# A fused Fourier-mixing and feed-forward block on one core: the second shift vector is summed in halves of 1024 columns, six of its sixteen units later, and two sums of mixing weights sooner

## The reference, cut to what matters

```python
mod_x = (silu(c) @ w_ada + b_ada)              # 2048 -> 6*2048
sh1, sc1, ga1, sh2, sc2, ga2 = split(mod_x, 6)
h = rmsnorm(x, g_mix) * (1 + sc1) + sh1
f = fftn(h.reshape(1, 512, 4, 512), axes=(1, 3), norm='ortho').real
x = x + ga1 * (f.reshape(1, 512, 2048) @ w_mix)
h2 = rmsnorm(x, g_ffn) * (1 + sc2) + sh2
x = x + ga2 * (square(relu(h2 @ w_in)) @ w_out)  # 2048 -> 8192 -> 2048
return rmsnorm(x, g_final)
```

## Time and profile before

| | us |
|---|---|
| median of 3 runs (lowest, highest) | 1658.37 (1655.5, 1659.79) |
| the profiled execution's own time | 1658.63 |
| its span | 1656.4 |
| PE busy, share of the span | 1602.9 (97%) |
| DVE busy | 1263.7 (76%) |
| ACT busy | 545.5 (33%) |
| clock of PE, mean of the span | 0.99 of full |

### The profile page before, as it was taken

The page is one execution under the profiler, slowest core; times in us unless marked ns, Lnnn a source line. Parts: engine busy times, 40 slices in busy tenths (PEclk is TensorE's granted clock), DMA queues, the critical chain, the costliest instruction groups (busy, mean ns, idle before and its releaser), DMA issues.

```text
span 1656.4 us, 18306 instructions
## 1 busy us (share of the span) xinstructions
PE 1602.9 (97%) x6989; PEld 1232.9 (74%) x6989; DVE 1263.7 (76%) x1148; ACT 545.5 (33%) x658; POOL 16.8 (1%) x30
## 2 busy tenths in 40 slices
PE   6899989899999999999999999999999999999996
PEld 5653323688888888888888888888888888888875
DVE  6649998448888888886868686867677777777878
ACT  5320002443333333333333333333333333333332
POOL 0000000100000000000000000000000000000000
PEclk9999999999999999999999999999999999999998
DMA  9999998713535454432323232322323333333342
GB/s 356 369 394 374 413 350 347 274 52 113 193 121 184 130 175 137 143 127 78 125 82 120 93 110 101 101 101 101 101 101 101 101 101 101 101 103 100 116 189 102
DMA packets 94921, 272.63 MB, mean 165 GB/s; under 512 B 4332, under 2 KB 5660, under 8 KB 80924
## 3 DMA queue, kind: packets, MB, share of 16 engines
q1 hardware_dynamic: 91616, 249.91, 42.1%
q0 software_dynamic: 3120, 22.07, 3.7%
q10 hardware_dynamic: 144, 0.07, 0.0%
HBM read 263.64 MB, written 8.39 MB: 164 GB/s over the span
## 4 chain that ended last, share of the span: by engine, by line
PE 86%; DVE 9%; DMA 2%; issue 2%; ACT 0%; SPq 0%; DVEq 0%; POOL 0%; ACTq 0%
PE banks L1234 16%; PE banks L1236 16%; PE banks L1235 16%; PE banks L1534 11%; PE banks L1538 11%; PE banks L1536 11%; DVE acc_a L802 4%; DVE acc_b L802 2%; DMA raw<-in_w_ada 1%; DVE mixw L900 1%; PE banks L1467 1%; PE banks L1252 1%; DMA xres<-in_x 0%; DVE gated L955 0%; DVE xres L959 0%
## 5 line engine op out<-in xcount | busy, mean ns | idle before, releaser
L1092 DVE TENSOR_TENSOR stp<-raw,stp 128x1024 fp32r<-128x1024 f32 x330 | 402.5, 1223 | 156.8 <-ACT stp L673 154.3
L673 ACT ACTIVATE stp<-raw 128x1024 fp32r<-128x1024 f32 x330 | 343.7, 1056 | 523.4 <-PE banks L1236 233.9
L1234 PE MATMUL banks<-acts,stp 128*128 128x512 f32 x1024 | 399.6, 390 | 0.0
L1235 PE MATMUL banks<-acts,stp 128*128 128x512 f32 x1024 | 398.4, 389 | 0.0
L1236 PE MATMUL banks<-acts,stp 128*128 128x512 f32 x1024 | 398.4, 389 | 0.0
L1538 PE MATMUL banks<-stp,hid 128*128 128x512 f32 x840 | 326.8, 389 | 0.0
L1536 PE MATMUL banks<-stp,hid 128*128 128x512 f32 x840 | 326.8, 389 | 0.0
L1534 PE MATMUL banks<-stp,hid 128*128 128x512 f32 x840 | 326.8, 389 | 0.0
L1113 DVE TENSOR_TENSOR dacc<-dacc,banks 128x1024 f32<-128x1024 f32 x202 | 245.8, 1217 | 14.2 <-PE banks L1538 14.2
L1236 PEld LDWEIGHTS banks<-acts,stp 128*128 128x128 f32 x1024 | 192.2, 188 | 40.0
L1234 PEld LDWEIGHTS banks<-acts,stp 128*128 128x128 f32 x1024 | 192.3, 188 | 39.7 <-DVE stp L1092 0.3
(11 more groups left out here) (185 smaller groups left out, 1210.1 us busy)
## 6 DMA issues: line engine op xcount, KB each, us to landing
raw<-in_w_ada SPq DMA_DIRECT2D x80, 1024.0 KB, 7.7
raw<-in_w_ffn_in SPq DMA_DIRECT2D x64, 1024.0 KB, 5.8
raw<-in_w_ffn_out SPq DMA_DIRECT2D x64, 1024.0 KB, 5.0
mixw<-in_w_mix SPq DMA_DIRECT2D x16, 1024.0 KB, 9.4
gate_w<-in_w_ada POOLq DMA_DIRECT2D x16, 1024.0 KB, 5.2
xres<-in_x SPq DMA_DIRECT2D x4, 1024.0 KB, 9.9
xmix_d<-xres POOLq DMA_DIRECT2D x4, 1024.0 KB, 11.3
xmix<-xmix_d SPq DMA_DIRECT2D x4, 1024.0 KB, 8.0
```

Of the source, the lines that this page charges most:

```text
L673: nc.scalar.activation(stp[:, slot, 0, :, :], source.rearrange("p (a n) -> p a n", a=2), ACT.Copy).then_inc(w_hi, 1)
L1092: nc.vector.tensor_tensor(stp[:, slot, 1, :, :], source.rearrange("p (a n) -> p a n", a=2), stp[:, slot, 0, :, :].bitcast(F32), ALU.subtra ...
L1234: nc.tensor.matmul(bank, w_hi_ap, m_hi, start=first, stop=False)
L1235: nc.tensor.matmul(bank, w_hi_ap, m_lo, start=False, stop=False)
```

## The change

Shift 2 no longer comes as 16 units of one row block by 2048 columns, but as 16 units of two row blocks by 1024 columns: 8 units for the left half b = 0, 8 for the right half. Ten of them are loaded and summed in the mixing stage, after scale 2, and six in the prelude. Each takes two DVE instructions on 1024 columns. A half is summed over partitions on PE by eight matmuls with one column (`shift2_sums`), without a copy on ACT and without transposes, and added to its bias on DVE (`shift2_mods`). The first half is needed before the first `hmod`, the second before k = 8.

`mix_sums(1)` moves ahead of the gate steps of n = 0, `mix_sums(14)` ahead of the combine and update after n = 13. Scale 2's row is finished ahead of the diagonal of the norm's factors. Up unit 1 and up steps 2 and 3 move to the end of the mixing stage. `turn_tokens` uses 3 banks and is 2 ahead, not 4 and 3.

```diff
-    others = [("ada", j, k) for j in (GATE1, SHIFT2, SCALE2) for k in range(DT)]
-    between = [3] + [2] + [3] * 11 + [2] + [3] + [LATE]
+    early_shift2 = 10
+    S_ROWS, S_COLS = 2, UNIT // 2
+    shift2 = [("shift2", b, q) for b in range(D // S_COLS) for q in range(DT // S_ROWS)]
+    others = [("ada", j, k) for j in (GATE1, SCALE2) for k in range(DT)]
+    others[-LATE:-LATE] = shift2[:early_shift2]
+    between = [3, 2, 3, 3, 3, 2] + [2] * 6 + [3] * 3 + [LATE]
...
-        units += [("up", 0)] * (i == len(mix_units) - 1) + runs[-1]
+        units += [("up", 0), ("up", 1)] * (i == len(mix_units) - 1) + runs[-1]
...
-    units += up_units[1:]
+    units += shift2[early_shift2:] + up_units[2:]
+    SUM_BANKS = (3, 7)
+    TURNS = 3
+    AHEAD = UPDATED[-1] + 1
...
+            def shift2_unit(w):
+                ...
+                for i in range(S_ROWS):
+                    k = S_ROWS * q + i
+                    source = raw[:, u % RAW, S_COLS * i:S_COLS * (i + 1)]
+                    if k == 0:
+                        nc.vector.tensor_scalar(acc, source, silu[:, 0:1], None, ALU.mult).then_inc(col_step, 1)
+                    else:
+                        dve.wait_ge(col_step, DT * b + k)
+                        nc.vector.scalar_tensor_tensor(acc, source, silu[:, k:k + 1], acc,
+                                                       ALU.mult, ALU.add).then_inc(col_step, 1)
...
             for n in range(MU):
-                if n >= 1:
+                if n == 0:
+                    mix_sums(1)
+                elif n not in (1, AHEAD):
                     mix_sums(n)
...
+                if n == AHEAD - 1:
+                    mix_sums(AHEAD)
...
-            up_low(0)
-            up_low(1)
+            for m in range(4):
+                up_low(m)
             update_pairs()
+            shift2_mods(0)
...
+                if k == S_TILES:
+                    shift2_mods(1)
                 dve.wait_ge(h2_hi, k + 1)
...
+                if early_shift2 + k < len(shift2):
+                    shift2_unit(shift2[early_shift2 + k])
...
             def late_step(i):
-                if i == 1:
-                    pe.wait_ge(gemv_step, SCALE1_STEPS + SHIFT1_STEPS + 2 * DT)
-                    add_share(3, acc_b, True).then_inc(col_sum, 1)
-                elif i == 3:
-                    turn_rows(3, 0)
                 gemv_rows(SCALE2, DT - LATE + i - 1)
...
+            def shift2_sums(b):
+                pe.wait_ge(col_step, DT * (b + 1))
+                for k in range(S_TILES * b, S_TILES * (b + 1)):
+                    mm = nc.tensor.matmul(banks[:, SUM_BANKS[b], k:k + 1], acc_b[:, P * k:P * (k + 1)], ones[:, 0:1],
+                                          start=True, stop=True, skip_group_check=True)
+                mm.then_inc(shift2_sum, 1)
...
-            LEAD = 3
+            LEAD = TURNS - 1
+            gemv_rows(SCALE2, DT - 3)
             gemv_rows(SCALE2, DT - 2)
             gemv_rows(SCALE2, DT - 1)
...
             add_share(1, acc_a).then_inc(col_sum, 1)
+            shift2_sums(0)
+            turn_rows(3, 2)
             pe.wait_ge(diag_ready, 1)
             turn_tokens(0)
-            turn_rows(4, 2)
```

More of the change, by code:

```diff
@@ L126, in prelude_slot @@
     def prelude_slot(m):
-        return (m + (2 if m < 2 else 3)) % SLOTS
+        return (m + 3) % SLOTS
     def slot_at(i):
@@ L351, in unit_source @@
                     return ada_v[:, w[2], w[1] * D:(w[1] + 1) * D]
+                if w[0] == "shift2":
+                    first = SHIFT2 * D + S_COLS * w[1]
+                    return ada_v[:, S_ROWS * w[2]:S_ROWS * (w[2] + 1), first:first + S_COLS]
                 if w[0] == "up":
@@ L360, in consumed @@
                     return gemv_pe, pe_order.index(w) + 1
+                if w[0] == "shift2":
+                    return col_step, S_ROWS * (shift2.index(w) + 1)
                 if w[0] == "ada":
@@ L515, in rows_of @@
                 nc.scalar.activation((rows if i < 3 else rows_late)[:, 0:width],
-                                     banks[:, (4, 5, 5, 3, 1)[i], 0:width], ACT.Copy)\
+                                     banks[:, (4, 5, 5, 1)[i], 0:width], ACT.Copy)\
                     .then_inc(rows_out, 1)
@@ L598, in _ @@
             up_high(1)
-            rows_of(3)
+            up_high(2)
+            up_high(3)
             act.wait_ge(x_updated, DB - 1)
@@ L607, in _ @@
             block_squares(1, DB - 1, DB, (0, 2))
+            rows_of(3)
             block_squares(1, DB - 1, DB, (1, 3))
@@ L610, in _ @@
             nc.scalar.activation(rms[:, 1, :], mean[:, 1, :], ACT.Sqrt).then_inc(rms_done, 1)
-            rows_of(4)
             act.wait_ge(mod_step, MODS_READY)
             for k in range(DT):
-                if k % 2 == 1 and k // 2 + 2 < UPS:
+                if k % 2 == 1 and 4 <= k // 2 + 2 < UPS:
                     up_high(k // 2 + 2)
+                if k % S_TILES == 0:
+                    act.wait_ge(mod_step, MODS_READY + k // S_TILES + 1)
                 act.wait_ge(h2_turned, k + 1)
@@ L619, in _ @@
                     act.wait_ge(h2_lo, k - 1)
-                nc.scalar.activation(hmod[:, k % 2, :], banks[:, 4 + k % 4, :], ACT.Identity,
+                nc.scalar.activation(hmod[:, k % 2, :], banks[:, 4 + k % TURNS, :], ACT.Identity,
                                      scale=mods[:, SCALE2, k:k + 1],
@@ L984, in update_pairs, with shift2_mods @@
                                             ALU.add).then_inc(pair_updated, 1)
-            def run_gemvs(n, first=0, last=DT):
-                for _, j, k in runs[n][first:last]:
-                    gemv(j, k)
+            def shift2_unit(w):
+                u = position[w]
+                _, b, q = w
+                acc = acc_b[:, S_COLS * b:S_COLS * (b + 1)]
+                dve.wait_ge(raw_full[u % RAW], filled[u])
+                for i in range(S_ROWS):
[7 more added lines that the diff above has]
+                                                       ALU.mult, ALU.add).then_inc(col_step, 1)
+            def shift2_mods(b):
+                dve.wait_ge(shift2_sum, b + 1)
+                tiles = slice(S_TILES * b, S_TILES * (b + 1))
+                nc.vector.tensor_tensor(mods[:, SHIFT2, tiles], banks[:, SUM_BANKS[b], tiles],
+                                        vec_t[:, SHIFT2 * DT + S_TILES * b:SHIFT2 * DT + S_TILES * (b + 1)],
+                                        ALU.add).then_inc(mod_step, 1)
+            def run_gemvs(n, first=0, last=DT):
+                for w in runs[n][first:last]:
+                    if w[0] == "shift2":
+                        shift2_unit(w)
+                    else:
+                        gemv(w[1], w[2])
             for n in range(MU):
-                if n >= 1:
+                if n == 0:
+                    mix_sums(1)
+                elif n not in (1, AHEAD):
                     mix_sums(n)
@@ L1024, in _ @@
             dve.wait_ge(rows_turned, 4)
-            turned_rows(SHIFT2, 0)
-            dve.wait_ge(rows_turned, 5)
             turned_rows(SCALE2, 2)
-            dve.wait_ge(mod_step, MODS_READY - 1)
+            dve.wait_ge(mod_step, MODS_READY)
             times_gain(SCALE2, vec_t[:, 7 * DT:8 * DT])
             for k in range(DT):
-                if k % 2 == 1 and k // 2 + 2 < UPS:
+                if k % 2 == 1 and 4 <= k // 2 + 2 < UPS:
                     up_low(k // 2 + 2)
+                if k == S_TILES:
+                    shift2_mods(1)
                 dve.wait_ge(h2_hi, k + 1)
@@ L1462, in turn_tokens @@
             def turn_tokens(k):
-                if k >= 4:
-                    pe.wait_ge(hmod_done, k - 3)
+                if k >= TURNS:
+                    pe.wait_ge(hmod_done, k - TURNS + 1)
                 for t in range(TT):
-                    mm = nc.tensor.matmul(banks[:, 4 + k % 4, P * t:P * (t + 1)],
+                    mm = nc.tensor.matmul(banks[:, 4 + k % TURNS, P * t:P * (t + 1)],
                                           xres[:, t, P * k:P * (k + 1)], diag[:, t, :], start=(t == 0), stop=True,
@@ L1488, in up_step @@
                     if first:
+                        if k == S_TILES - 1:
+                            shift2_sums(1)
                         if k + LEAD < DT:
```

21 lines of the change are left out of this document (11 added, 10 removed).

## The result

| | before | the change |
|---|---|---|
| median of the runs on the same chip (lowest, highest), us | 1659.35 (1655.18, 1660.77), 15 runs | 1663.27 (1661.49, 1667.0), 15 runs |
| ratio to before, 95% interval | 1 | 1.0031 [1.0024, 1.0038] |
| span of the profiled execution, us | 1656.4 | 1660.7 |

The change is slower by 0.31%, about 5 us; 1651.9 was forecast, with a range up to 1657. The span grew by 4.3 us.

The account below looks back on a forecast made before the run. PE bounds the prelude and 500 to 1589 us; in the mixing stage neither PE nor DVE alone. Terms -5.8 - 2.5 - 3.1 + 2.4 = -9.0, plus clock 1.4 + 1.0, gave -6.6 us: 1651.9 us, range 1647.5 to 1657.

Parts of the forecast that it names:

- What bounds the kernel: PE is always busy in the prelude and from 500 to 1589 us; earlier savings or losses carry to the end unchanged.
- `mix_sums(1)` ahead: Mixing stage: unit 0's even part starts at 132.2, not 129.50 us; unit 1 starts 1.9 us late, costing time.
- Six units out of the stage: Mixing stage: moving six shift 2 units out lets unit 15 start at 276.4, not 282.19 us: -5.8 us.
- Unit 15 shorter: Last mixing unit: shift 2's sum and transposes and one scale 2 unit leave its 16.9 us: -2.5 us.
- The hand-over: Unit 15's end to the prelude's first product: 11.2 us where it was 14.3: -3.1 us.
- The prelude's own additions: Prelude on PE: one more tile turn, +0.9 us, and eight one-column sums, 1.5 us; together +2.4 us.
- The clock: Slow PE after waits: 1.4 us at unit 0, 0.5 each before unit 15 and the diagonal; -9.0 becomes -6.6 us.
- are hidden, as long as their data is there: Prelude: six shift 2 units on DVE, 6 x 2.5 us, fit between remainders within PE's 3.6 us per tile.
- rival 3: Prelude starves: up unit 2 lands late beside POOL's transfers, PE waits for tile 5; +4 to +7 us, 1664; chance 0.08.

Follow-up runs that it names:

- b: The change with up unit 2 loaded two places sooner, ahead of shift 2's last two units; 1661.27 us, 1.0016 of before.
- e: The change with all 16 units of shift 2 summed in the mixing stage and none in the prelude; 1672.69 us, 1.0090 of before.
- a: The change with POOL's write of x and gate 2's first unit held until six prelude tiles have their remainders; 1654.59 us, 0.9983 of before.
- c: The change with only gate 2's first unit (1 of POOL's 5 MB) held until six prelude remainders; 1660.83 us, 1.0017 of before.
- g: The change with shift 2's first six units loaded and summed before scale 2's in the mixing stage; 1657.03 us, 0.9986 of before.
- h: The change with both edits, the held-back POOL transfers of a and the shift 2 order of g; 1649.78 us, 0.9944 of before.
- f: The change with `mix_sums(1)` back behind gate 1's third step, as before; 1660.21 us, 1.0012 of before.
- i: The edits of h plus `mix_sums(1)` back in its earlier place, as in f; 1646.17 us, 0.9926 of before.

## Why the prediction was wrong

**What bounds the kernel: right.** What was gained or lost up to the prelude's end was carried on unchanged, +4.31 us at the first product of the second map and +4.3 in the span.

**`mix_sums(1)` ahead: right in kind.** Unit 1 was issued at 111.37 and landed 11.1 us later, at 122.49 and not 124.2, so the even part of unit 0 started at 130.43, not 132.2. PE waited 1.93 us for it, not 3.7, and that was luck of this execution: PE had been late itself. Its first four records of unit 0, at 110.86 us, took 3.62 us at the low clock, and 3.7 to 3.8 in b and e. In the four other profiles with this order (a, c, g, h) they took 1.98; there the sums started 1.6 us later against the common start, and PE waited 3.5 to 3.6 us. That the edit costs time is supported by f and i, and the size was about right: 1.9 and 1.4 of slow clock were counted, 3.3 us, and f and i give 3 and 3.6 by the runs.

**Six units out of the stage: right.** DVE stood 8.51 us (7 forecast) for gate 1's sums, PE waited 0.30 at unit 10 (under 1), and unit 15 started at 277.76 (276 to 278). That hit is partly luck. With its slow clock at unit 0 the forecast had the release at 188.8 and unit 15 at 277.8; the release came at 187.34, and DVE's chain then took 90.4 us and not 88.9, since a half step took 1.33 us, not 1.25. So PE waited 3.16 us before unit 15, not 1.8.

**Unit 15 shorter: right at full clock.** g's 14.40 us is 16.9 - 2.5. The change took 16.1.

**The hand-over.** From unit 15's end to the first product it took 12.3 us (11 to 12.5 forecast).

**The prelude's own additions: right.** +2.7 in a, e and i (62.7 against 60.0) against 2.4; the sums took 1.8, not 1.5. The estimate by the Trainium skill (TensorE: Matmul & The Clock Gate, "LDWEIGHTS (loading the stationary operand)"), 1.7, was nearer to the trace.

**The clock: too low.** I counted 0.5 us each for the waits before unit 15 and before the diagonal. The first cost 1.7 (16.1 against 14.4). At the second, 24 turn records took 4.57 us where three turns at 0.9 are 2.7, and the hand-over came out at 12.3 instead of 11.2 + 0.5. Over what was counted that is 1.2 and 0.6 us, and it turns -9.0 (clock included, without the prelude's +2.4) into -7.3.

**The step that failed** is the sentence that the six units in the prelude "are hidden, as long as their data is there". The data was not there, and 8.9 of the 10.9 us between the forecast of -6.6 and the span's +4.3 are this: 5.8 us of wait for tile 5 and 3.0 of slow clock after it. Run a shows it: the same order with POOL's 5 MB held back has no wait and is a little faster than before (0.9983, interval to 0.9997). It is rival 3, and its mechanism was written out: the 13th unit, the write of x, tile 5, 1664 us. What was wrong was its chance, 0.08, and the rows were at hand. I had worked out that it decides from a landing of 6 us on, and the earlier trace rows has a median of 8.2 us for the busy stretch. The only reason against it was that the three loads are spread over 7 us, which says nothing of what else is in flight. The stretch with the write is in the trace of before, and I did not use it. There are SP's loads issued from 300 to 306 us, when the write begins, then POOL's transfers from 306 to 325 (KB each, us to landing):

```profile
raw<-in_w_ffn_in SPq DMA_DIRECT2D x2, 1024.0 KB, 7.8
...
xmix_d<-xres POOLq DMA_DIRECT2D x2, 1024.0 KB, 13.4
gate_w<-in_w_ada POOLq DMA_DIRECT2D x1, 1024.0 KB, 16.3
```

The 7.8 is the median of two: the load issued between 300 and 301 us took 5.9 us, and the next, issued between 301 and 302, took 9.7; the write began at 304.60. POOL's own transfers took 13 to 16 us, though SP issued no further load into `raw` until 322.51. So a landing of over 6 us was to be expected, and rival 3 should have been the forecast.

Within rival 3, two sizes were off and partly cancelled. I let three slow landings add up, 10 to 12 us of wait; only the last one counts, because units 15 and 16 are not what up unit 2's slot waits for. Its threshold was nearly right: landings of 5.3, 9.8 and 12.6 us (a, c, the change) gave waits of 0, 2.76 and 5.83, so about 1 us for each us from 6.8 to 7.0 on. And the slow clock cost 3.0, not 1.4.

The Trainium skill (DMA: Bandwidth & Descriptors, "Issuing engines are not separate DMA queues") says that transfers issued by several engines run on the same 16 DMA engines and interleave there. The runs agree: the landing of SP's unit rose from 5.3 to 12.6 us with POOL's 5 MB beside it, and with 4 MB it was 9.8. Whether the engines or the memory behind them are what is short, no run here shows.

What stays open: whether the write could go out sooner than in a without harm (not tried); the size of what `mix_sums(1)` ahead costs (by the traces, up to unit 15, it is 1.7 us between f and the change, where PE waited 1.93 us at unit 0, and 4.1 between i and h, where it waited 3.58); and why one wait costs more clock than another of the same length.

## What to carry to other kernels

Work that is moved to a quiet engine brings its loads with it: before it is counted as hidden, find the load that its ring of buffers delays, set its latest landing against the landing times of that very stretch, and take the slowest if a bulk write is in flight there. Delay the bulk write, which nobody waits for, rather than reorder the loads. And when a chain starts late on a released buffer, put work in front that doesn't need the buffer; here that was worth 0.45% by the ratios, and holding back the write 0.48%; by the traces 4.6 us and 8.9.

## What the runs showed of the hardware that was not expected

- The same wait did not always cost the same clock. After 3.2 us before unit 15 the low clock cost 1.7 us in the change, a and b, but about 5 in c and f (unit 15 took 19.4 and 19.0 us against 14.4 at full clock). After 7.97 us in e it cost 2.1.
- In the prelude a wait of 2.76 us cost 0.3 us of slow clock (c), 4.37 cost 1.8 (b), and 4.8 to 5.8 cost 2.7 to 3.0 (the change, f, g), each as the prelude's length over 62.7 less the wait.
- Waits of 1.9 us were followed by a slow stretch: before the even part of unit 0 (the change, four matmul records in 2.72 and not 1.98 us) and before the diagonal, where the 24 turn records took 4.3 to 5.5 us in all nine profiles behind the change (8 take 0.9 at full clock).
- A low clock can hide a late landing. Mixing unit 1 landed 11.0 to 11.1 us after its issue in the change, b and h and 10.2 in e, but its sums started 0.2 to 1.4 us after the common start in the change, b and e, where four of PE's records ahead of it had taken 3.6 to 3.8 us, and 3.0 to 3.1 us after it in a, c, g and h, where these had taken 1.98.
- 16 records with 128 weight columns and one column streamed took 1.8 us to the next instruction, whether in the change (297.46 to 299.26) or in i.
